# Two transfers instead of one for the first expert's rows, with half of its transposes moved

## The reference, cut to what matters

```
hf = rmsnorm(x, norm_g)                               # 576 rows of 1024
g_sel = top group of 4; top_i = top 2 of its 4 experts
gates (T, 16): two entries per token are not zero
for e in range(16):
    act = silu(hf @ w_gate[e]) * (hf @ w_up[e])       # 1024 -> 256
    y = y + (act * gates[:, e:e+1]) @ w_down[e]       # 256 -> 1024
x = x + y
```

## Time and profile before

| what | value |
|---|---|
| median of 3 runs | 827.15 us |
| profiled execution, span from first to last instruction | 823.5 us |
| profiled execution, its own time | not recorded apart from the span; the median lies 3.6 us above the span |
| PE busy | 808.6 us, 98% of the span |
| DVE, ACT, POOL busy | 600.6, 478.4, 320.3 us |
| chain that ended last | PE 90%, DVE 4%, DMA 3% |
| granted clock of TensorE, mean | 0.998 |

### The profile page before, as it was taken

How to read it: one execution, slowest core, us unless ns; L and a number is a source line. 1 busy time by engine, 2 the same in 40 slices (tenths; PEclk the granted TensorE clock), 3 DMA queues, 4 the chain that set the end, 5 groups by cost and what they waited for, 6 DMA issues and landing times.

```text
span 823.5 us, 11871 instructions
## 1 busy us (share of the span) xinstructions
PE 808.6 (98%) x4070; PEld 651.3 (79%) x4070; DVE 600.6 (73%) x957; ACT 478.4 (58%) x810; POOL 320.3 (39%) x207
## 2 busy tenths in 40 slices
PE   9999999999999999999999999999999999999995
PEld 6887788888868888888588887888878678888871
DVE  5444655645689999999854456555747899999986
ACT  5533342513478888887663432442334798888874
POOL 0016994301042345664100299913011322665540
PEclk9999999999999999999999999999999999999999
DMA  9732223223949999998853222221278699999867
GB/s 308 269 111 77 71 71 115 92 76 130 411 169 359 382 354 382 395 375 295 267 194 101 73 78 76 64 90 65 84 285 328 207 416 359 382 384 391 339 234 281
DMA packets 57295, 188.18 MB, mean 229 GB/s; under 512 B 10862, under 2 KB 11886, under 8 KB 49036
## 3 DMA queue, kind: packets, MB, share of 16 engines
q1 hardware_dynamic: 44476, 156.57, 52.5%
q0 software_dynamic: 10368, 23.09, 7.6%
q10 hardware_dynamic: 2400, 7.87, 2.5%
HBM read 173.00 MB, written 29.39 MB: 246 GB/s over the span
## 4 chain that ended last, share of the span: by engine, by line
PE 90%; DVE 4%; DMA 3%; issue 1%; ACT 1%; POOL 0%; ACTq 0%; SPq 0%; POOLq 0%; DVEq 0%
PE ps L485 13%; PE ps L1455 12%; PE ps L1457 12%; PE ps L1456 12%; PE ps L489 10%; PE ps L488 10%; PE ps L1463 3%; PE ps L487 3%; PE ps L1434 2%; PE ps L1654 1%; PE ps L1715 1%; DMA hg<-xn_d,rowidx 1%; PE ps L1679 1%; PE ps L1694 1%; PE ps L1405 1%
## 5 line engine op out<-in xcount | busy, mean ns | idle before, releaser
L485 PE MATMUL ps<-wh,hT 128*128 128x512 f32 x408 | 163.5, 401 | 0.2
L898 POOL DMA_INDIRECT y_d<-y,rowidx x32 | 111.8, 3493 | 125.8 <-DVE y L2179 124.5
L2154 DVE TENSOR_TENSOR gul<-wgu,eh 128x1024 fp32r<-128x1024 f32 x128 | 150.1, 1212 | 0.1
L2145 DVE SCALAR_TENSOR_TENSOR wl<-raw,gcol,wh 128x512 fp32r<-128x512 f32 x80 | 78.5, 984 | 75.3 <-ACT wh L1107 75.2
L1138 ACT ACTIVATE eh<-wgu 128x1024 fp32r<-128x1024 f32 x128 | 128.4, 1058 | 3.7 <-PE ps L1457 3.7
L489 PE MATMUL ps<-wh,lT 128*128 128x512 f32 x313 | 122.4, 391 | 0.0
L488 PE MATMUL ps<-wl,hT 128*128 128x512 f32 x313 | 121.9, 390 | 0.0
L1455 PE MATMUL ps<-eh,hgTh 128*128 128x512 f32 x240 | 96.6, 403 | 0.4 <-issue 0.4
L1457 PE MATMUL ps<-eh,hgTl 128*128 128x512 f32 x240 | 93.9, 391 | 0.0
L1456 PE MATMUL ps<-gul,hgTh 128*128 128x512 f32 x240 | 93.6, 390 | 0.0
L1107 ACT ACTIVATE wh<-raw,gcol 128x512 fp32r<-128x512 f32 x80 | 57.3, 719 | 59.8 <-PE ps L487 57.6
(11 more groups left out here) (271 smaller groups left out, 1688.2 us busy)
## 6 DMA issues: line engine op xcount, KB each, us to landing
wgu<-in_gate_up SPq DMA_DIRECT2D x64, 1024.0 KB, 12.4
wdn<-in_w_down SPq DMA_DIRECT2D x64, 512.0 KB
raw<-in_w_in SPq DMA_DIRECT2D x79, 256.0 KB, 2.7
raw<-in_w_out SPq DMA_DIRECT2D x32, 256.0 KB, 2.9
back<-y_d SPq DMA_DIRECT2D x16, 512.0 KB, 5.5
s<-in_state_ret POOLq DMA_DIRECT2D x8, 512.0 KB, 4.0
xn_d<-xf ACTq DMA_DIRECT2D x8, 512.0 KB, 6.6
x_in<-in_x_cols SPq DMA_DIRECT2D x8, 288.0 KB, 5.2
```

The source lines that it names most:

```text
L485: pe.matmul(out, both, w_h, start=first, stop=False)
L898: pool.indirect_dma_start(out=y_d, out_offset=bass.IndirectOffsetOnAxis(ap=rowidx[:, 1, e:e + 1], axis=0), in_=y[s][:, :], in_offset=None, ...
L2145: ve.scalar_tensor_tensor(out=wl[S % SPL][:, :], in0=raw[S % RAW][:, :], scalar=gcol[:, 0, L, s % KC:s % KC + 1], in1=wh[S % SPL][:, :].bi ...
L2154: ve.tensor_tensor(gu_pair(gul, gul3, e, s, p), gu_pair(wgu, wgu3, e, s, p), gu_split(e, p)[:, :].bitcast(F32), ALU.subtract).then_inc(glo, 1)
```

## The change

The first expert's rows come in two transfers, each of 512 of the 1024 columns. For this the table is viewed as 1152 half rows, and two more DVE instructions write `halfidx`, the row number times two plus 0 or 1, ahead of `rowidx`. The left half has a semaphore of its own, `gat_left`; the right half uses `gat[0]`.

PE now waits for the left half alone and makes its four transposes. The right half's four transposes, with their wait for `gat[0]`, stand in `early_gu` between the eight products with high rows and the four with low rows.

A third edit concerns the start of the program: the semaphore `still_set` is gone, and PE's 11 idle turns wait for `ready0` instead, which is complete only when all four fills are done.

```
+            def gather_half(e, half, sem):
+                cols = slice(512 * half, 512 * half + 512)
+                pool.indirect_dma_start(out=hg[e % 3][:, cols], out_offset=None, in_=xn_d.rearrange("r (h d) -> (r h) d", h=2),
+                                        in_offset=bass.IndirectOffsetOnAxis(ap=halfidx[:, half:half + 1], axis=0),
+                                        bounds_check=half_bound, oob_is_err=False).then_inc(sem, 16)
...
-                pool.wait_ge(tidx_done, L + 1)
-                for e in range(3):
+                pool.wait_ge(tidx_done, 2 * L + 1)
+                gather_half(0, 0, gat_left)
+                gather_half(0, 1, gat[0])
+                pool.wait_ge(tidx_done, 2 * L + 2)
+                for e in (1, 2):
                     gather(e)
...
-            def rows_t(s, sem, pair=False):
-                for half in range(2):
+            def rows_t(s, sem, pair=False, halves=range(2)):
+                for half in halves:
...
+                if first(e):
+                    pe.wait_ge(gat[0], 16 * used(L, 0, 0))
+                    rows_t(0, t_mm, halves=(1,))
                 pe.wait_ge(hg_lo, X * 2 + 1)
...
-            pe.wait_ge(still_set, 1)
+            pe.wait_ge(ready0, 4)
             idle_turns(7, 11)
...
-                pe.wait_ge(gat[0], 16 * used(L, 0, 0))
-                rows_t(0, t_mm, pair=True)
+                pe.wait_ge(gat_left, 16 * (L + 1))
+                rows_t(0, t_mm, pair=True, halves=(0,))
...
+            for half in range(2):
+                last = ve.tensor_scalar(halfidx[:, half:half + 1], ps[2][:, 0:1], 2.0, 2.0 * NO_ROW + half, ALU.mult, ALU.add)
+            last.then_inc(tidx_done, 1)
...
-            ve.memset(still[:, :], 0.0).then_inc(still_set, 1)
+            ve.memset(still[:, :], 0.0)
```

More of the change, by code:

```diff
@@ L199, in build @@
         rowidx = tile("rowidx", [P, 2, NE], U32)
+        halfidx = tile("halfidx", [P, 2], U32)
         tab = region + 4096 * 3
@@ L331, in build @@
         gu3_ld = [sem(f"gu3_ld{h}") for h in range(2)]; dn3_ld = [sem(f"dn3_ld{k}") for k in range(2)]
-        gat = [sem(f"gat{i}") for i in range(3)]
+        gat = [sem(f"gat{i}") for i in range(3)]; gat_left = sem("gat_left")
         early_ld = [sem("early_ld0"), sem("early_ld1")]
@@ L337, in build @@
         out_st = sem("out_st")
-        ready0 = sem("ready0"); still_set = sem("still_set"); sq_done = sem("sq_done"); rms_done = sem("rms_done"); xn_done = sem("xn_done")
+        ready0 = sem("ready0"); sq_done = sem("sq_done"); rms_done = sem("rms_done"); xn_done = sem("xn_done")
         tr_done = sem("tr_done"); hi_done = sem("hi_done"); lo_done = sem("lo_done")
@@ L902, in _ @@
             row_bound = pool.to_reg(SEQ + NSAMP - 1)
+            half_bound = pool.to_reg(2 * (SEQ + NSAMP) - 1)
             y_bound = pool.to_reg(2 * TOK - 1)
```

## The result

The changed kernel took 829.27 us (median of 8 runs, 827.49 to 833.77), the kernel before 826.66 us beside it (8 runs, 824.97 to 827.21). The ratio is 1.0039, 95% interval 1.0022 to 1.0057: 3.2 us slower (1.8 to 4.7). The profiled execution, 827.49 us with a span of 825.7 us, is the fastest of the eight, and its span is 2.2 us over that of before. So the trace shows less of the loss than a typical run has. In every run here the time lies 1.7 to 1.9 us above the span; the other half of the 3.6 us between median and span of before is that the execution profiled there was quicker than the median.

The account below looks back on a forecast made before the run. PE, busy 98% of the span, was taken to bound the kernel. 0.85 + 0.78 + 0.2 = 1.8 us on the 823.5 us span gave 825.3; with 3.6 us from span to median, 829.0 us, range 827.5 to 830.2.

Parts of the forecast that it names:

- Left half, and the gain in front: First expert, each layer: left half lands in time, PE's transposes begin 0.40 us earlier, first products some 0.4 us earlier.
- Moved transposes and the new wait: First expert: moved transposes spend the 0.4 us won; `p` = 2 waits for right `hgTl`; loss 0.85 and 0.78 us.
- the 0.75: PE at `p` = 2, layer 0: forecast wait in us for the right half's `hgTl`.
- the 0.3 below which the forecast called itself wrong: PE at `p` = 2: a wait for DVE's `hgTl` missing or below 0.3 us would show the forecast wrong.
- The start: Program start: idle turns begin 1.19 us later, first true product 0.23 late; cost 0.2 us, ends 0 and 0.7.
- the rival of a dear start: Program start: the clock rises late, 0.5 us more, 829.5 us; chance 0.07.
- "A microsecond later hides.": SP behind the gathers: expert 3's loads start at 249.66, ACT first uses them at 273.39, so lateness costs nothing.
- "From there on the experts follow PE.": From the second expert's low products on: DVE is just in time, experts follow PE, the delay runs to the end.

Follow-up runs that it names:

- f_wait: Changed kernel with idle turns waiting for `still_set` again and expert 3's gate and up weights asked for before the gather waits: 828.03 us, ratio 1.0020.
- f_mid: Changed kernel with `still_set` back, expert 3's gate/up load early, right half's transposes behind four of eight high-row products: 826.48 us, ratio 1.0005.
- e1_start: Kernel before with only the idle turns changed, waiting for `ready0` instead of `still_set`: 827.29 us, ratio 1.0006.
- b_early: Kernel before with expert 3's gate and up weights asked for ahead of SP's waits for gathers and stores: 825.89 us, ratio 0.9996.
- b_dose: Kernel before with SP also waiting for expert 0's `act` ahead of expert 3's gate and up load: 833.21 us, ratio 1.0077.
- a_early: Changed kernel with expert 3's gate and up weights asked for ahead of SP's waits for gathers and stores: 828.75 us, ratio 1.0023.
- e3_right_first: Changed kernel with the right half's wait and transposes directly behind the left's, ahead of the products: 827.76 us, ratio 1.0012.
- e4_middle: Changed kernel with the right half's wait and transposes behind four of the eight high-row products: 828.66 us, ratio 1.0019.

## Why the prediction came out as it did

The place and the kind of the loss were right. The time, 829.27 for 829.0, was right partly by luck: the kernel before took 826.66 us beside the changed one and not 827.15, and with 3.2 us on top of 827.15 it would have been 830.4, above the range. The sum of 1.8 us was low against the measured 3.2 (1.8 to 4.7): one step of it was wrong, one term was missing, and one was too small.

*Left half, and the gain in front.* Right. It lands in time: PE's transposes at 243.06 wait for nothing. The transfers' rows (median us from issue to landing) show what no row showed before, 3.2 us for a half, against 4.4 for the whole:

```profile
hg<-xn_d,halfidx POOLq DMA_INDIRECT x2, 3.2
```

By the Trainium skill, DMA: Bandwidth & Descriptors (Anatomy of one DMA, the gpsimd path), half the bytes save an estimated 0.34 us; the trace has 1.2, and the measurement decides. It gave nothing more, since PE comes at 243.06 and ACT later still.

*Moved transposes and the new wait.* Right in place and, a little large, in size. From the first moved transpose to `p` = 2 it took 2.01 us in both layers (247.96 - 245.95, 653.65 - 651.64), for 2.1 to 2.15. The profile's waits, 0.48 and 0.28 us, can't be set against the 0.75, nor layer 1's against the 0.3 below which the forecast called itself wrong: they count from the end of the last low product, whose row is 0.39 long, while products follow each other every 0.23. Counted from when PE could have gone on, 0.16 earlier, they are 0.64 and 0.44. In layer 0 PE is there 1.37 us after the first moved transpose, as forecast. In layer 1 it is 0.2 later, since the low products start at 652.17, right behind the left half's `hgTl` (DVE's row ends at 652.12), which the prediction had not holding PE back. To `p` = 2 the loss is 0.65 and 0.57 us, with the slower first product (0.1) 0.75 and 0.67, for 0.85 and 0.78. That is 1.4 us over both layers for 1.6, and f_wait less f_mid, which differ by the place of the transposes alone, is 1.4 too.

*The start.* 0.08 us in the profiled run, and 1 us or more in others, for 0.2; the mean by e1_start is 0.5 (-0.3 to 1.4). My upper end of 0.7 was too low, and the rival of a dear start holds in a part of the executions. By the Trainium skill, TensorE: Matmul & The Clock Gate (Part 1), the moment of release differs from run to run; the traces agree, 6.83 against 8.28 for the same line of products.

*"A microsecond later hides."* This step failed. I looked at the load that SP issues next, expert 3's, and took its use to be 23 us away. That row was misread: ACT makes four instructions for each expert's weights, and by their count 273.39 belongs to expert 4. Expert 3's weights are used from 264.18, 14.5 us after the load:

```profile
264.18 2.98 ACT L1138 ACTIVATE eh<-wgu 128x1024 fp32r<-128x1024 f32 x3
```

For this load a microsecond does hide, ACT shows no wait there. But the transfers behind it queue up on full DMA engines. The kernel asks for the weights of experts 3, 6, 4 and 5 in this order, and the tight ones are the last, expert 5's, and the rows `back`. Their price is the difference between kernels with and without the early load: 3.2 - 1.9 = 1.3 us in the changed kernel, 2.8 - 1.7 = 1.1 with the old start. The intervals of each pair overlap; both pairs together give 1.2 us, with an interval of about 0.1 to 2.4. Part of it may be a gain of the early load itself, which starts 4 us ahead of where it stood before (b_early, 0.3 us, with an interval from -1.2 to 0.6). That lateness alone can cost time is shown by b_dose, where 2.6 us of it cost 6.4; that the changed kernel's 1.3 us of it cost 1.2 is argued.

*"From there on the experts follow PE."* They follow it 0.02 us slower each. The prediction had no term for this; it is the estimated 0.5 to 0.6 us of the fourth part above.

So 1.4 us are the new wait, which is shown by f_wait and f_mid and by the trace, and 0.5 to 0.6 the slower experts, which every trace with the split gather shows. About 1.2 for the late transfers and 0.5 for the start are differences of times that can't be fixed closer; all four together are 3.7, within the interval of the 3.2. What makes runs of the changed kernel differ by 6 us is open: a_early's eight runs lie within 2.6 us, which speaks for the late transfers, but 24 runs of the kernel before in that round differ by 5.5.

## What to carry to other kernels

A piece of work that hides in another engine's latency is only free there: before moving it, write down the chain that hangs on it, here 2.0 us of PE, ACT and DVE, and see whether what stands between covers it. When a step delays a queue of transfers, don't ask when the next transfer is used; follow the queue to the transfer with the least slack, as far as the DMA share stays near 1. And an input that comes earlier helps only if every engine behind it can take it up earlier; its in-order list decides, not the landing.

## What was not expected of the hardware

The start of TensorE has two forms with the same first idle turn. Turns of 0.43 us (1.2 GHz) change to 0.21 us (2.4 GHz) after about 5 us of the program in one execution, and in another PE is slow until about 8, both after an idle stretch of 2.2 us. The granted clock of these windows reads 1.00 in both, so here only the durations tell; between 5 and 6 us PE has four instructions under way in e1_start (first) and six in the changed kernel (second):

```profile
5.00:6.00 1.00, 1.00 (x4) 0.31 (x3) 0.96 (x3) 0.57 (x1) 0.00 (x0) 1.00 1.06 337
```

```profile
5.00:6.00 1.00, 1.00 (x6) 0.55 (x5) 0.96 (x3) 0.63 (x1) 0.00 (x0) 1.00 1.06 367
```

And lateness on full DMA engines can cost more than its own length: in b_dose 2.6 us at the load's issue in layer 0, and as much in layer 1, cost 6.4. It is no rule: in e3_right_first and e4_middle the load starts 2.7 and 2.4 us later than before, and all their losses together are 1.0 and 1.6 us.
